# Attention with q in two layouts, by token and by residue modulo 4

## The reference

```
h = rmsnorm(x);  q, k, v, g, z, xbc, dt = split(h @ w_in)        # 2048 x 1024 each for q, k, v
q, k = rmsnorm per head of 64
for window, d in (128, 1), (512, 4), (2048, 16):                 # three patterns
    each query reads the keys at distances 0, d, 2d, ..., window, backwards only
    s = q . k * 64**-0.5 + bias[bucket(distance)];  o, lse = softmax(s) @ v, logsumexp(s)
o = the three o, weighted by softmax over their lse;  a = silu(g) * o
```

## Time and profile before

| | us |
|---|---|
| median of 3 runs | 2953.14 |
| lowest, highest | 2942.0, 2957.29 |
| the profiled execution | 2948.5 |
| its span in the trace | 2946.8 |
| `project` ends, first load of `attend` issued at | 1369.5 |
| first score product at | 1393.5 |
| last score product at | 2107.4 |
| TensorE busy, of the span | 2685.3 (91%) |
| VectorE, ScalarE, GpSimd busy | 1241.8, 884.7, 888.9 |

### The profile page before, as it was taken

One profiled execution on the slowest core, in us unless ns is written; L12 is line 12 of the kernel. 1 busy time (PEld: TensorE's weight loads), 2 busy tenths in 40 slices (PEclk: granted clock), 3 DMA queues, 4 the chain that ended last, 5 costly groups with the idle time before them and its releaser, 6 DMA issues. The chain is left out here.

```text
span 2946.8 us, 43683 instructions
## 1 busy us (share of the span) xinstructions
PE 2685.3 (91%) x16598; PEld 2368.1 (80%) x16598; DVE 1241.8 (42%) x3366; ACT 884.7 (30%) x1933; POOL 888.9 (30%) x711
## 2 busy tenths in 40 slices
PE   7899999999999999996899999999934999986999
PEld 6899999999998888883799899988833777764675
DVE  3245554445000015441565556656515555543321
ACT  3312122222111111111355545545614444432000
POOL 1045454512121213211023344333441333321510
PEclk9999999999999999997999999999976999997999
DMA  4224345566232111114556666657345655535851
GB/s 156 83 74 114 103 127 154 150 184 183 67 101 90 71 57 71 44 43 122 127 117 135 148 149 139 149 115 161 89 102 158 184 183 184 181 109 192 320 181 70
DMA packets 198556, 382.27 MB, mean 130 GB/s; under 512 B 62379, under 2 KB 119955, under 8 KB 184500
## 3 DMA queue, kind: packets, MB, share of 16 engines
q1 hardware_dynamic: 156916, 229.77, 25.8%
q0 software_dynamic: 38784, 145.28, 18.7%
q10 hardware_dynamic: 2672, 4.74, 0.5%
HBM read 259.94 MB, written 125.15 MB: 131 GB/s over the span
## 5 line engine op out<-in xcount | busy, mean ns | idle before, releaser
L118 PE MATMUL bank<-w_hi,hT_hi 128*128 128x256 f32 x1792 | 508.2, 284 | 14.2 <-DMA ident<-ident 11.3
L120 PE MATMUL bank<-w_hi,hT_lo 128*128 128x256 f32 x1792 | 505.0, 282 | 0.0
L119 PE MATMUL bank<-w_lo,hT_hi 128*128 128x256 f32 x1792 | 503.6, 281 | 0.0
L1179 PE MATMUL front<-k_hi,q_st 128*128 128x256 f32 x768 | 316.5, 420 | 42.6 <-DMA k_lo<-qk 29.0
L118 PEld LDWEIGHTS bank<-w_hi,hT_hi 128*128 128x128 f32 x1792 | 339.1, 189 | 15.1 <-DMA ident<-ident 11.6
L1222 PE MATMUL obank<-turned_p,v_in 128*128 128x128 f32 (+1 forms) x1632 | 322.5, 331 | 23.8 <-ACT turned_p L1355 22.8
L120 PEld LDWEIGHTS bank<-w_hi,hT_lo 128*128 128x128 f32 x1792 | 339.5, 189 | 0.0
L119 PEld LDWEIGHTS bank<-w_lo,hT_hi 128*128 128x128 f32 x1792 | 339.0, 189 | 0.0
L1222 PEld LDWEIGHTS obank<-turned_p,v_in 128*128 128x128 f32 x1632 | 271.8, 198 | 43.0 <-ACT turned_p L1355 25.8
L1342 ACT ACTIVATE score<-score,ntop_sb 128x256 f32<-128x256 f32 (+1 forms) x768 | 289.9, 455 | 5.5 <-DMA ntop_t<-ntop 5.3
L1180 PE MATMUL front<-k_lo,q_st 128*128 128x256 f32 x768 | 274.2, 365 | 0.0
(11 more groups left out here) (299 smaller groups left out, 4980.6 us busy)
## 6 DMA issues: line engine op xcount, KB each, us to landing
qk<-xc_in SPq DMA_DIRECT2D x64, 512.0 KB, 5.1
w_raw<-w_in POOLq DMA_DIRECT2D x26, 1024.0 KB, 7.0
q_st<-qk POOLq DMA_DIRECT2D x32, 512.0 KB, 8.7
k_hi<-qk POOLq DMA_DIRECT2D x32, 512.0 KB, 11.7
k_lo<-qk POOLq DMA_DIRECT2D x32, 512.0 KB, 14.7
v_in<-v_out POOLq DMA_DIRECT2D x16, 1024.0 KB, 12.7
cum_all<-cum SPq DMA_DIRECT2D x16, 1024.0 KB, 9.8
xcT<-xc SPq DMA_DIRECT2D x12, 1024.0 KB, 3.9
```

The costliest lines, as they stand in the source:

```text
L118: pe.matmul(out, lhs_hi(k), rhs_hi(k), start=k == 0, stop=False)
L119: pe.matmul(out, lhs_hi(k), rhs_lo(k), start=False, stop=False)
L120: last = pe.matmul(out, lhs_lo(k), rhs_hi(k), start=False, stop=k == KT - 1)
L1179: pe.matmul(out, lhs, with_axes(k_hi[:, b, 0:1], axes, first), start=True, stop=False)
```

## The change

`project` also writes q in a second layout. For the 16 q groups and each half c, ScalarE copies the table once more with the tokens sorted by residue modulo 4 (`take_high_by_four`), VectorE subtracts in the same order (`take_low_by_four`), and SP stores the two parts, one DMA of 256 KB each, to a new scratch tensor `q4` (`store_by_four`). Both halves of a group go through one buffer, `q4_parts`, which lies in `stage`. Half 0 is handled with the dense parts; half 1 one or two tiles later: ScalarE after tile 4u + 8, VectorE and SP after tile 4u + 9.

`attend` keeps q in two single buffers, `q_by[0]` by token and `q_by[1]` by residue. The dense pattern reads the first; the middle one reads `q_by[1]` without stride, the widest one with stride 4. k is as before. Every load of q and k is one DMA to 128 partitions: q's high and low rows in one, k's rows read twice. GpSimd's order has changed with it.

```
+            q4_parts = stage[:, :, :].rearrange("p a w -> p (a w)").rearrange("p (x w) -> p x w", x=2)
+            by_four = lambda ap: ap.rearrange("p (i r) -> p r i", r=4)
...
 pe, turn(u), before the transposes of half c:
+                        if 1 <= u <= QK_GROUPS // 2:
+                            pe.wait_ge(q4_split, 2 * (u - 1) + c + 1)
 act:
+                        if c == 0 and u < QK_GROUPS // 2:
+                            take_high_by_four(u, c)
+                def take_high_by_four(u, c):
+                    if 2 * u + c >= 1:
+                        act.wait_ge(q4_stored, 32 * (2 * u + c))
+                    if c == 1:
+                        act.wait_ge(qk_split, 2 * u + 2)
+                    act.copy(fours(q4_parts[:, 0, :].bitcast(F32R)), by_four(tables[c][:, :])).then_inc(q4_high, 1)
...                         in the loop over n, after the square:
+                    if n % RING == 0 and 1 <= n // RING - 1 <= QK_GROUPS // 2:
+                        take_high_by_four(n // RING - 2, 1)
 dve:
+                def take_low_by_four(u, c):
+                    dve.wait_ge(q4_high, 2 * u + c + 1)
+                    dve.tensor_tensor(fours(q4_parts[:, 1, :].bitcast(F32R)), by_four(tables[c][:, :]), fours(q4_parts[:, 0, :]),
+                                      ALU.subtract).then_inc(q4_split, 1)
...                         in the loop over n, after the scaling:
+                    if n % RING == 1 and 1 <= n // RING - 1 <= QK_GROUPS // 2:
+                        take_low_by_four(n // RING - 2, 1)
 sp:
+                def store_by_four(u, c):
+                    sp.wait_ge(q4_split, 2 * u + c + 1)
+                    for x in range(2):
+                        dst = bass.AP(tensor=scr["q4"].tensor, offset=(x * D + slab * SLAB + c * P) * SEQ + P * quad,
+                                      ap=[[SEQ, P], [512, 4], [1, P]])
+                        sp.dma_start(dst, fours(q4_parts[:, x, :])).then_inc(q4_stored, 16)
...
 attend, gpsimd:
+            def load_k(h):
                 if h >= 2:
                     pool.wait_ge(front_ready, scores_end[h - 2])
+                for dst, x in ((k_hi, 2), (k_lo, 3)):
+                    pool.dma_start(dst[:, h % 2, :].bitcast(F32), head_rows(x, h, 0)).then_inc(k_loaded[h % 2], 16)
+            def load_q(h):
+                if h >= 1:
+                    pool.wait_ge(front_ready, scores_end[h - 1])
+                pool.dma_start(q_by[0][:, :].bitcast(F32), head_rows(0, h, D * SEQ)).then_inc(q_loaded, 16)
+            def load_q4(h):
+                if h >= 1:
+                    pool.wait_ge(front_ready, unit_done(h - 1, 2 * UNITS // 3 - 1))
+                pool.dma_start(q_by[1][:, :].bitcast(F32), head_rows(0, h, D * SEQ, "q4")).then_inc(q4_loaded, 16)
...
+            load_q4(0)
+            load_k(0)
+            load_q(0)
+            load_k(1)
...                         then load_q4(1), load_v(2), load_q(1), load_v(1), load_v(0), load_k(2), load_q4(2)
...                         in the loop over h, after the wait for ntop:
+                if h + 2 < H:
+                    load_q(h + 2)
+                if h + 3 < H:
+                    load_k(h + 3)
...                         and after the loads of v and the reciprocal, before normalise(h - 1):
+                if h + 3 < H:
+                    load_q4(h + 3)
 tensor:
+                    pe.wait_ge(k_loaded[b], 32 * (h // 2 + 1))
+                    pe.wait_ge(q4_loaded, 16 * (h + 1))
+                if 2 * UNITS // 3 in units:
+                    pe.wait_ge(q_loaded, 16 * (h + 1))
...
-                        lhs = with_axes(q_st[:, b, 0:1], [[d, P]], P * d * blk + r)
+                        if p == 2:
+                            lhs = with_axes(q_by[1][:, 0:1], [[4, P]], 4 * P * (r % 4) + r // 4)
+                        else:
+                            q_at = (P * blk, 4 * P * r + P * blk)[p]
+                            lhs = q_by[p][:, q_at:q_at + P]
```

More of the change, by code:

```diff
@@ L365, in project @@
             qk_stored = [sem(f"qk_stored{c}") for c in range(2)]
+            q4_high, q4_split, q4_stored = sem("q4_high"), sem("q4_split"), sem("q4_stored")
             mhalf_set = sem("mhalf4_set")
@@ L639, in take_low @@
                         dve.wait_ge(qk_high, 2 * u + c + 1)
+                        if c == 0 and u < QK_GROUPS // 2:
+                            dve.wait_ge(q4_high, 2 * u + 1)
                         dve.tensor_tensor(qk_parts[:, 1, c, :].bitcast(F32R), tables[c][:, :], qk_parts[:, 0, c, :],
                                           ALU.subtract).then_inc(qk_split, 1)
+                        if c == 0 and u < QK_GROUPS // 2:
+                            take_low_by_four(u, c)
+                def take_low_by_four(u, c):
+                    dve.wait_ge(q4_high, 2 * u + c + 1)
+                    dve.tensor_tensor(fours(q4_parts[:, 1, :].bitcast(F32R)), by_four(tables[c][:, :]), fours(q4_parts[:, 0, :]),
+                                      ALU.subtract).then_inc(q4_split, 1)
                 for n in range(NORM):
@@ L724, in store_qk @@
                         sp.dma_start(dst, qk_parts[:, :, c, :]).then_inc(qk_stored[c], 16)
+                        if c == 0 and u < QK_GROUPS // 2:
+                            store_by_four(u, c)
+                def store_by_four(u, c):
+                    slab, quad = u // 4, u % 4
+                    sp.wait_ge(q4_split, 2 * u + c + 1)
[3 more added lines that the diff above has]
+                        sp.dma_start(dst, fours(q4_parts[:, x, :])).then_inc(q4_stored, 16)
                 for s in range(QK_SLABS):
@@ L734, in _ @@
                             store_qk(n // RING - 1)
+                        if t % RING == 1 and 1 <= n // RING - 1 <= QK_GROUPS // 2:
+                            store_by_four(n // RING - 2, 1)
                     sample_store(s, 0)
@@ L741, in _ @@
                     sp.wait_ge(qk_stored[c], 16 * QK_GROUPS)
+                sp.wait_ge(q4_stored, 32 * QK_GROUPS)
                 sp.wait_ge(s_stored, 16 * (QK_SLABS + 1))
@@ L917, in attend @@
         ident = sb("ident_a", [P, P])
-        q_st = sb("q_st", [P, 2, SEQ], F32R)
+        q_by = [sb(f"q_by{d}", [P, SEQ], F32R) for d in DILATIONS[:2]]
         k_hi = sb("k_hi", [P, 2, SEQ], F32R)
@@ L941, in attend @@
         const_in = sem("const_in")
-        qk_loaded = [sem(f"qk_loaded{b}") for b in range(2)]
+        k_loaded = [sem(f"k_loaded{b}") for b in range(2)]
+        q_loaded, q4_loaded = sem("q_loaded"), sem("q4_loaded")
         v_loaded = [sem(f"v_loaded{p}") for p in range(3)]
@@ L1098, in _, with head_rows, unit_done @@
         def _(pool):
-            def load_qk(h):
+            def head_rows(x, h, apart, of="qk"):
+                first = scr[of][x, h * HD:(h + 1) * HD, :]
+                return bass.AP(tensor=first.tensor, offset=first.offset, ap=[[SEQ, HD], [apart, 2], [1, SEQ]])
+            def unit_done(h, u):
+                return place["score", h, u] + 1
+            def load_k(h):
                 if h >= 2:
                     pool.wait_ge(front_ready, scores_end[h - 2])
[L1103 to L1106, removed]
+                for dst, x in ((k_hi, 2), (k_lo, 3)):
[8 more added lines that the diff above has]
+                pool.dma_start(q_by[1][:, :].bitcast(F32), head_rows(0, h, D * SEQ, "q4")).then_inc(q4_loaded, 16)
             def apply_gate(h, b, pair):
@@ L1130, in _ @@
             pool.wait_ge(ones_set, 4)
-            for p in (2, 1, 0):
+            load_q4(1)
+            load_v(pool, 2, 0)
+            load_q(1)
+            for p in (1, 0):
                 load_v(pool, p, 0)
-            load_qk(2)
+            load_k(2)
+            load_q4(2)
             for h in range(H):
@@ L2451 @@
     "qk": (4, D, SEQ),
+    "q4": (2, D, SEQ),
     "z": (SEQ, D),
```

5 lines of the change are left out of this document (1 added, 4 removed).

## The result

The changed kernel takes 2973.9 us (median of 5 runs, 2973.0 to 2979.1) against 2952.7 us (5 runs) before: ratio 1.0084, 95% interval 1.0061 to 1.0106. It is slower by 21 us.

| from | to | before, us | after, us | difference |
|---|---|---|---|---|
| start | first load of attention issued (end of the projections) | 1369.5 | 1428.9 | +59.4 |
| there | first product of the mix (`back`) | 79.5 | 76.9 | -2.6 |
| there | last product of the mix | 714.9 | 683.2 | -31.7 |
| there | end | 782.9 | 782.3 | -0.6 |

A forecast was written before the change was run, and what follows sets the result against it. TensorE was taken to set the pace in projection and attention. Projection +65, products -17 + 4, start -5, chain and q by four -7 gave +40 us on 2948.5 or 2953.1: forecast 2990 us, range 2932 to 3045.

The forecast's parts named there:

- Projection: Projection of q: both halves share one buffer, so two store landings in series stretch each group to 17.3 us; +65 us.
- the steps: One q group: half 0 subtracted 1.28, landed 6.6, half 1 subtracted 9.7, landed 14.3, next group's scaling done 17.3 us.
- the signs that I gave: Projection: ScalarE waits of 2 to 4 us on by-four stores, group period near 17 us, TensorE idle, then lower clock.
- Products: Score products in attention, 14 heads: middle pattern gains 17 us from dense q, widest pattern loses 4 us.
- The reading of the moving operand: Score products: strided k as moving operand alone holds TensorE's array for about 0.2 us, whatever q's layout.
- the 7 first loads per head: Middle pattern: the first q weight load of each of 7 lots gets 0.10 us cheaper; 0.7 us per head.
- the other 25 products: Middle pattern, products after each lot's first: pace falls from 0.24 to 0.22 us; 0.5 us per head taken.
- Start: Attention's first loads: TensorE's 29.0 us wait for head 0 shortens with full-width loads; 5 us gained (0 to 10).
- Chain and q by four: Attention: reciprocal's small DMAs finish sooner, against late by-four q loads; 25 gained to 25 lost, 7 us gained taken.
- Quick landings: Projection rival: by-four stores land within about 3.5 and 2.5 us, costing at most 20; 2925 us, chance 0.2.
- q as the bound of the middle pattern: Score-product rival: q's stride sets the middle pattern's pace, gaining 3.7 us per head; 2955 us, chance 0.08.
- q by four late: Attention rival: by-four q arrives 2.5 us late on heads with two v loads; 3018 us, chance 0.17.

The follow-up runs named there:

- Experiment 3: Changed kernel, but each half of q has its own by-four buffer (low part stored twice, high part left out): 2923.7 us, ratio 0.9903.
- experiment 8: Changed kernel with k read densely, 256 columns in a row, in every score product (wrong values for the strided patterns): 2940.8 us, one run.
- experiment 9: Kernel before with k read densely, 256 columns in a row, in every score product, q strided as before: 2939.5 us, one run.
- experiment 1: Kernel before with only the loads changed: three of 1 MB to 128 partitions per head instead of six of 512 KB to 64: 2907.7 us, ratio 0.9853.
- experiment 6: Changed kernel with each load of q and k issued as two over 64 partitions, layouts and load order kept: 3058.8 us, ratio 1.0378.
- experiment 7: Kernel before with its six 512 KB loads per head cut by columns, so each covers 128 partitions: 2915.4 us, ratio 0.9882.

## Why the prediction was right, and where its terms were off

The forecast was slower, 2990 us in 2932 to 3045; 2974 came, by the forecast's mechanism: the projection pays for two landings in series, attention gives back less. That the time came so near is in part luck: against the sum of +40 the chain was 22 us better and the projection 6, the products 10 worse and the start 2.

- **Projection, +65 predicted, +59.4 measured.** From the start of VectorE's subtraction the steps were 1.28, 6.6, 9.7, 14.3 and 17.3 us. The traced group has 1.3, 6.2 (268.04), 9.1 (end of the low part of half 1), 12.6 (274.47) and 15.3. But it is the quickest one. Over all sixteen the average is 16.7 us, so 17.3 was 0.6 too long, and the landings are enough to explain it: from issue to ScalarE's copy half 0's stores took 4.9 us on average where I had 5.3, half 1's 4.2 where I had 4.6. The split within TensorE was off: 42.3 us of idle and 17.1 of products at a lower clock (0.95 in the stretch, where it was 1.00), where I had 60 and 5. The 17.1 need not be a cost of their own. VectorE, ScalarE and the stores set the period, and TensorE fills part of it with slow work instead of idling; what the clock adds by itself no run shows. Of the signs that I gave, the period near 17 us came; ScalarE's waits are 5.0 us on average, not 2 to 4. Experiment 3 shows the series itself: the same work in two buffers costs 3.6 us.
- **Products, -17 + 4 predicted, -2.7 measured** (mix of 683.2 us against 685.9 with wide loads alone). The reading of the moving operand held (experiments 8, 9), and so did the 7 first loads per head: 0.11 us each, since the second product of the lot now starts 0.28 us after the first, 0.39 before. What failed is the 0.5 us per head for the other 25 products: their pace stayed at 0.233 to 0.24. The widest pattern took 0.017 us more per product, 0.54 a head, near the upper end of the 0 to 0.6 that I gave it. Together that is 14 x (0.8 + 0.1 - 0.54) = 5 us gained, 2.7 in the runs.
- **Stride 4.** The row showed stride 4 as dear as stride 16; the changed kernel and experiment 8 bear that out with a pace of 0.234 us. By the rule of the Trainium skill (SBUF — State Buffer, section Door 1: The DMA port swizzle) that four float32 can be strided for free, the widest pattern should have gained; it lost. The first half of that rule, two accesses per 16-byte line for full rate, fits in that every product with a strided operand is slower here than one with both dense; it doesn't say why stride 16 is slightly quicker than stride 4.
- **Start, -5 predicted, -3.3 to the first score product and -2.6 to the first product of the mix.** With wide loads alone it is -5.6 and -11.5. One reason is in the trace: the second head's first product waits 5.2 us (at 1478.28) for q by token, which has one buffer and is asked for only when the first head is scored (1472.25); and `scores`, where a head is scored in one piece as the first two are, waits for it ahead of all units, though only the last third reads it. I had looked at that wait only for heads scored in pieces. Moving it was not tried.
- **Chain and q by four, -7 predicted, -29.0 measured.** This is the term most mis-sized. I had set "up to 25 can go" against "up to 25 lost" for a late q by four and taken a value near the middle. The gain came whole (experiment 1: -29.0 in the mix, the waits for `turned_p` down from 18.9 to 2.6 us), and the loss didn't come (0.7 us). With narrow loads the changed kernel has hardly any waits for `turned_p` either, but then the loss comes (experiment 6).
- **The sum.** +59.4 - 29.0 - 2.7 - 2.6 = +25.1, against +24.5 between the spans.
- **The rivals.** Quick landings: refuted, the period is 16.7 us on average and never under 15.3, and ScalarE goes on 4.2 to 6.0 us after the issue of half 0's stores, 3.5 to 5.2 after half 1's, where the rival needed 3.5 and 2.5. q as the bound of the middle pattern: refuted, 0.233 with dense q. q by four late: not in this kernel, but real. With half-width loads it costs 56.7 us of waits at the very place I named, heads with two loads of v. What keeps it away is the wide loads, which I had priced at nothing ("the engines are as busy as before"): in the mix the DMA share fell from 0.56 to 0.52 while the rate rose from 129 to 156 GB/s.

The best version is wide loads with nothing else of the change: 2907.7 us, 43.5 under the kernel before in the same series (2951.3). Even with a buffer per half the second layout doesn't pay: experiment 3, with the changed attention and the same stores, took 2923.7 us in that series, 16 more.

## What to carry to other kernels

A side task that is small as busy time can still set the pace when its one buffer is emptied by a DMA before the next step in program order may run. Count the landings in series around the loop, and give each its own buffer before anything else. One traced round of such a loop can be an unusual one; take the average over all of them. A layout that makes one operand of a product dense pays only where the other is dense as well. And time the parts of a change one by one: here one of its three parts was worth -44 us, and another hid it at +57.

## What the runs showed of the hardware

- Loads that cover 128 partitions move more with less engine time than loads of 64. At equal bytes and count, over the mix, it is 134 GB/s at a DMA share of 0.48 against 129 at 0.56 (experiment 7 and the kernel before); with half as many loads of twice the size, from 1540 to 2100, 169 at 0.56 against 151 at 0.66 (the changed kernel and experiment 6). The Trainium skill (DMA: Bandwidth & Descriptors, section Rules for kernel authors) advises one transfer over 128 partitions instead of two over the halves, and the times bear it out. A factor of two between them isn't seen in any stretch here.
- 256-column products with one or both operands strided start 0.22 to 0.24 us apart, 0.12 us with both dense; as weights stride 16 is slightly quicker than stride 4 (0.22 against 0.23, experiment 9).
- Stores of 512 KB in runs of 512 bytes that share the queue with dense stores in 2 KB runs let ScalarE go 4.2 to 6.0 us after their issue (4.9 on average), the same bytes in 2 KB runs after 5.7 to 8.4 (6.5).
- The reciprocal's 8 KB store among loads of 64 partitions kept SP waiting 10.2 us on average (132.5 us in 13 waits), among loads of 128 partitions 5.8 us (75.4 in 13; the kernel before and experiment 1).
- Behind a wait of 1.88 us TensorE's granted clock was 0.50 from 257.00 to 259.60 and 1.00 from 259.70 on: 14 products in 2.6 us, then 47 in 5.3.
